# High weights that move the high and the low part of 256 tokens in one matmul of 512 columns

## The chip, the cores and the metric

The kernel runs on one core of one Trainium2 chip, in one launch. The metric is the device time in microseconds (us); lower is better. The engines that matter here are TensorE (PE; its weight loads are PEld in the profile), VectorE (DVE), ScalarE (ACT), and the DMA queue of SyncE (SP). Each engine works through its own list of instructions in order, and semaphores tie the lists together.

## The reference, cut to what matters

Two blocks of a transformer on 256 tokens (the second with 256 tokens of context beside them), D = 1024, in float32. The change concerns the two feed forwards that run on the 256 tokens alone: the one at the end of the first block, and the very last one of the program.

```python
def swiglu(xn, w_ffn_in, w_ffn_out):            # first block
    gate, up = jnp.split(xn @ w_ffn_in, 2, axis=-1)
    return (jax.nn.silu(gate) * up) @ w_ffn_out   # 1024 -> 2 x 2816 -> 1024
h = h + swiglu(rmsnorm(h, norm2_w), w_ffn_in, w_ffn_out)

# last feed forward of the second block
x = x + 0.5 * mx[8] * swiglu_2(modulate(rms_norm(x), mx[6], mx[7]), *ffn2)
```

The other feed forwards run on tokens and context together (512 columns).

## The kernel before

**Numbers in two parts.** Every operand of a large matmul is kept as a high part (rounded to the type fp32r) and a low part (the rest). A product is three matmuls into the same sums: high weights by high x, high weights by low x, low weights by high x (`product`, line 344). Each matmul has its own weight load.

**Weights.** All weights come in chunks of 512 KB, eight tiles of 128 x 128, in one stream through a ring of RING = 6 slots. SP loads chunk c+6 once TensorE has used chunk c (`load_chunk`, L286). ScalarE casts a chunk to its high part (`split_hi`, L292), then VectorE subtracts to get the low part (`split_lo`, L298). Both do this LEAD = 3 chunks ahead: in step i of a stage each engine first splits chunk i+3 and then reads the sums that end with chunk i. TensorE waits for `lo_ready` before a chunk.

**The feed forward.** `ffn` makes two stages. `FfnUp` has 44 blocks of 128 features, gate and up blocks in turn, each with eight k tiles, so one chunk makes one block: 44 chunks. `IntoResid` (down) has 8 blocks with 22 k tiles each: 22 chunks. So a feed forward is 66 chunks or 528 tiles, 1584 matmuls of 256 columns. The sums rotate over BANKS = 3 banks of psum: block b waits until the bank of block b-3 has been read.

**Reading the sums.** After a gate block ScalarE writes `raw = silu(psum)` (L571). After an up block VectorE multiplies, `raw = raw * psum` (L582), ScalarE casts that to the high part of the hidden tile (L574), and VectorE subtracts to the low part (L584). In the down part VectorE adds each of the eight blocks into `resid` (L439 without a gate, L446 with one), and then sums squares (L454 to L457).

**Which feed forwards.** With 256 tokens the tile set is `hidden_x`. The first one (feed forward 1 below) is interleaved, chunk by chunk, with the stage `Modulation(1)`: its own 512 KB chunks, matmuls on L715, and per round a ScalarE copy (L726), two transposes (L707) and a VectorE addition (L737). The last one (feed forward 2) stands alone near the end of the program; after it come transposes and the store of the result. The norm ahead of each writes `normed` tile by tile.

Of the kernel before, what the change touches and what calls it, by code (L numbers as in the profile page):

```python
# [13 lines left out]
P = 128  # L14
S = 256
# [153 lines left out]
def build(nc, W, consts, where, out):  # L169
    with ExitStack() as ctx:  # L170
# [6 lines left out]
        def raw_hi_lo(name, *free):  # L177

            start = -(-nc.sbuf_base // 32) * 32
            raw = sb(name + "_raw", *free)  # L180
            hi_at[name] = -(-nc.sbuf_base // 32) * 32
# [3 lines left out]
        hi_at = {}  # L185
# [18 lines left out]
        normed_raw, *normed = raw_hi_lo("normed", KD, 2 * S)  # L204
        under_hi = nc.alloc_sbuf_tensor_at("under_normed_hi", [P, KD, 2 * S], F32, offset=hi_at["normed"])
# [12 lines left out]
        hidden_x = [at(KF * S, KF, S), *split_at("hidden_x", (0, KF * S), KF, S)]  # L218
# [9 lines left out]
        def row(name):  # L228
# [33 lines left out]
                  "single": 0, "sub": 0, "evac_act": 0, "evac_dve": 0, "merged": 0}  # L262
# [84 lines left out]
        class LinearF(Stream):  # L347
# [8 lines left out]

            def tensor(self, pe, i):
                c = self.first + i
                pe.wait_ge(lo_ready, c + 1)
                for q in range(CT * i, CT * (i + 1)):  # L360
# [5 lines left out]
                    j = q % CT  # L366
                    last = self.product(psum[:, self.bank(b), 0:self.w], c, slice(j * P, (j + 1) * P), False,
# [54 lines left out]
        class IntoResid(LinearF):  # L422
# [11 lines left out]
            def evac_vector(self, dve, step, i):  # L434
                for k in self.ended(i):
                    dve.wait_ge(used, self.first + i + 1)
                    r = resid[:, k, self.a]
                    if self.gate is None:
# [113 lines left out]
        class FfnUp(LinearF):  # L552
# [7 lines left out]
            def parts(self, h):  # L560
                return [t[:, h, :] for t in self.pair]
# [4 lines left out]
            def evac_scalar(self, act, step, i):  # L566
                for b in self.ended(i):
                    raw, hi, _ = self.parts(b // 2)
# [7 lines left out]
            def evac_vector(self, dve, step, i):  # L576
                for b in self.ended(i):
                    raw, hi, lo = self.parts(b // 2)
                    if b % 2 == 1:
                        dve.wait_ge(*bank_free[self.group + b - 1])  # L580
                        dve.wait_ge(used, self.first + i + 1)
                        ve.tensor_tensor(raw, raw, self.sums(b), ALU.mult).then_inc(evac_dve, 1)  # L582
                        dve.wait_ge(hid_hi, self.hid0 + b // 2 + 1)
                        ve.tensor_tensor(lo, raw, hi.bitcast(F32), ALU.subtract).then_inc(hid_ready, 1)  # L584
# [1502 lines left out]
        def ffn(up, down, tiles, a, pair, gate, norm):  # L2087

            first = FfnUp(up, tiles, a, pair)
            first.ready = norm.ready  # L2090
            second = IntoResid(down, tiles, pair[1:], slice(0, a.stop - a.start), gate)
            second.ready = first.hidden_ready
# [324 lines left out]
```

## Time and profile before

| what | us |
|---|---|
| median of 3 runs | 2839.81 (2838.78 to 2842.81) |
| the profiled execution | 2841.48 |
| its span (first to last instruction) | 2839.7 |
| PE busy in the span | 2596.8 (91%) |
| DVE busy | 1378.9 (49%) |
| ACT busy | 1044.0 (37%) |
| granted TensorE clock, mean | 0.954 of full speed |
| feed forward 1, from its second chunk to its last matmul | about 592 to 829 |
| feed forward 2, likewise | about 2643 to 2831 |

The profile's page counts a matmul as busy from its start until its result has drained, so consecutive matmuls overlap in it. The distance between the starts of two matmuls is the better measure of what one costs in a stream. A line of a timeline reads: start, duration, engine, line of the kernel, operation, what is written and read, and in brackets the idle time before it with what ended it.

### The profile page before, as it was taken

To read this page: it belongs to the slowest core of one execution; us is meant where nothing else is said; L and a number is where in the kernel's file an instruction comes from. 1 tells how busy PE (TensorE), PEld (TensorE's weight loads), DVE (VectorE), ACT (ScalarE), POOL (GpSimd) and SP (SyncE) were. 2 spreads that over 40 slices of the span, in tenths; PEclk is the share of its full clock that TensorE was granted. 3 is DMA by queue.
4 is the path that set the end of the run, shared out by engine and by line. 5 is a ranking of instruction groups with operands and counts; after the bars stand their busy time and mean duration, and the time that the engine had idled before them with its cause. 6 is when DMAs were issued, how large, how long until landed. Compare 5 with 4: busy or idle time off the path is not lost. (4 is left out here: it accounts for less than half of the span.)

```text
span 2839.7 us, 36318 instructions
## 1 busy us (share of the span) xinstructions
PE 2596.8 (91%) x15294; PEld 2159.7 (76%) x15294; DVE 1378.9 (49%) x2279; ACT 1044.0 (37%) x1628; POOL 0.2 (0%) x4
## 2 busy tenths in 40 slices
PE   5999899899989999989888999989999896758999
PEld 5887679878867888867666888868888784446898
DVE  3746454554444333367865333343333354556654
ACT  3534454433333222245542222132222243344443
POOL 0000000000000000000000000000000000000000
PEclk8999999999999999989989999999999997769999
DMA  6886643488842222335002322322222243021454
GB/s 229 273 253 207 207 134 111 134 303 301 295 155 83 98 98 98 97 117 167 1 23 75 98 98 98 98 76 96 97 96 97 89 150 94 1 74 39 160 182 140
DMA packets 145188, 372.36 MB, mean 131 GB/s; under 512 B 20202, under 2 KB 65794, under 8 KB 144898
## 3 DMA queue, kind: packets, MB, share of 16 engines
q1 hardware_dynamic: 144402, 367.82, 40.2%
q8 instruction: 122, 2.00, 0.3%
q10 hardware_dynamic: 624, 2.21, 0.2%
q14 instruction: 40, 0.33, 0.0%
HBM read 368.84 MB, written 1.15 MB: 130 GB/s over the span
## 5 line engine op out<-in xcount | busy, mean ns | idle before, releaser
L298 DVE TENSOR_TENSOR weights_lo<-weights_raw,weights_hi 128x1024 fp32r<-128x1024 f32 (+1 forms) x545 | 656.1, 1216 | 536.0 <-ACT weights_hi L292 533.8
L344 PE MATMUL psum<-normed_hi,weights_hi 128*128 128x256 f32 (+1 forms) x2560 | 866.8, 339 | 38.5 <-DVE normed_lo L543 28.1
L344 PE MATMUL psum<-normed_lo,weights_hi 128*128 128x256 f32 (+1 forms) x2560 | 847.3, 331 | 0.0
L344 PE MATMUL psum<-normed_hi,weights_lo 128*128 128x256 f32 (+1 forms) x2560 | 846.7, 331 | 0.0
L292 ACT CAST weights_hi<-weights_raw 128x1024 fp32r<-128x1024 f32 (+1 forms) x545 | 562.0, 1039 | 382.3 <-DMA weights_raw<-in_w_down 267.3
L344 PEld LDWEIGHTS psum<-normed_hi,weights_hi 128*128 128x128 f32 x2560 | 488.7, 191 | 136.5 <-issue 67.3
L344 PEld LDWEIGHTS psum<-normed_lo,weights_hi 128*128 128x128 f32 x2560 | 490.0, 191 | 43.7 <-issue 1.2
L344 PEld LDWEIGHTS psum<-normed_hi,weights_lo 128*128 128x128 f32 x2560 | 489.4, 191 | 44.4
L344 PE MATMUL psum<-hidden_hi,weights_hi 128*128 128x512 f32 x528 | 205.4, 389 | 0.0
L344 PE MATMUL psum<-hidden_lo,weights_hi 128*128 128x512 f32 x528 | 205.4, 389 | 0.0
L344 PE MATMUL psum<-hidden_hi,weights_lo 128*128 128x512 f32 x528 | 205.4, 389 | 0.0
L344 PE MATMUL psum<-weights_hi,normed_hi 128*128 128x512 f32 (+2 forms) x400 | 151.4, 379 | 27.4 <-DVE weights_lo L298 14.9
L446 DVE SCALAR_TENSOR_TENSOR resid<-psum,mod,resid 128x256 f32<-128x256 f32 x80 | 35.8, 481 | 273.5 <-PE psum L344 273.5
L582 DVE TENSOR_TENSOR arena<-arena,psum 128x512 f32<-128x512 f32 (+1 forms) x110 | 63.9, 581 | 209.4 <-PE psum L344 209.4
L574 ACT CAST hidden_hi<-arena 128x512 fp32r<-128x512 f32 x66 | 40.9, 620 | 309.3 <-DVE arena L582 309.3
L571 ACT ACTIVATE arena<-psum 128x512 f32<-128x512 f32 (+1 forms) x110 | 56.3, 512 | 250.1 <-PE psum L344 250.0
L344 PE MATMUL psum<-weights_hi,normed_lo 128*128 128x512 f32 (+2 forms) x400 | 147.5, 369 | 0.0
L344 PE MATMUL psum<-weights_lo,normed_hi 128*128 128x512 f32 (+2 forms) x400 | 147.2, 368 | 0.0
L344 PEld LDWEIGHTS psum<-weights_hi,normed_hi 128*128 128x128 f32 x400 | 81.4, 204 | 46.6 <-issue 18.3
L344 PEld LDWEIGHTS psum<-hidden_hi,weights_lo 128*128 128x128 f32 x528 | 99.1, 188 | 20.7
L344 PEld LDWEIGHTS psum<-hidden_hi,weights_hi 128*128 128x128 f32 x528 | 99.1, 188 | 20.5
L344 PEld LDWEIGHTS psum<-hidden_lo,weights_hi 128*128 128x128 f32 x528 | 99.1, 188 | 20.5
(290 smaller groups left out, 2886.5 us busy)
## 6 DMA issues: line engine op xcount, KB each, us to landing
weights_raw<-in_w_gu SPq DMA_DIRECT2D x220, 512.0 KB, 3.5
weights_raw<-in_w_down SPq DMA_DIRECT2D x110, 512.0 KB, 3.5
arena<-in_w_mod SPq DMA_DIRECT2D x72, 512.0 KB, 5.5
resid<-in_w_mod SPq DMA_DIRECT2D x24, 512.0 KB, 5.2
normed_raw<-in_w_mod SPq DMA_DIRECT2D x24, 512.0 KB, 5.5
under_normed_hi<-in_w_mod SPq DMA_DIRECT2D x24, 512.0 KB, 5.3
weights_raw<-in_w_x SPq DMA_DIRECT2D x24, 512.0 KB, 4.5
weights_raw<-in_w_qk SPq DMA_DIRECT2D x24, 512.0 KB, 3.8
```

Of the source, the lines that this page charges most:

```text
L292: se.copy(w_hi[:, c % RING, a], w_raw[:, c % RING, a]).then_inc(hi_ready, 1)
L298: ve.tensor_tensor(w_lo[:, c % RING, a], w_raw[:, c % RING, a], w_hi[:, c % RING, a].bitcast(F32), ALU.subtract).then_inc(lo_ready, 1)
L344: last = te.matmul(out, a, b, start=start and n == 0, stop=stop and n == 2)
L446: last = ve.scalar_tensor_tensor(out=resid[:, k, mine], in0=psum[:, self.bank(k), side * S - at0:(side + 1) * S - at0], scalar=mod[:, m, s ...
L571: se.activation(raw, self.sums(b), ACT.Silu).then_inc(evac_act, 1)
L574: se.copy(hi, raw).then_inc(hid_hi, 1)
L582: ve.tensor_tensor(raw, raw, self.sums(b), ALU.mult).then_inc(evac_dve, 1)
```

## The change

In both feed forwards of 256 tokens, high and low part of x now lie side by side in memory (`normed_parts`, `hidden_parts`), and the high weights move both in one matmul of 2 x 256 columns. The low weights then move the high part alone (256 columns). Per tile there are two matmuls and two weight loads where there were three of each. The sums of a block therefore stand as two halves of one bank, to be added on the way out:

- Up part (`FfnUpHalves`): ScalarE copies one half to SBUF (`hid_half`), VectorE adds the other half (`evac_dve`). For a gate block ScalarE then applies silu to that sum (`hid_silu`). For an up block VectorE multiplies both (`hid_gate`), ScalarE casts the product to the high part, VectorE subtracts to the low part.
- Down part: two VectorE instructions for each block, one per half, with a wait between them, in place of one.

The feed forwards of 512 columns keep `FfnUp` and three matmuls. The layout of `normed` changes for all (low and high part of a k tile alternate), not what is read of it.

```diff
 # LinearF.tensor
+                    if self.parts is not None:
+                        a, bank = slice(j * P, (j + 1) * P), self.bank(b)
+                        te.matmul(psum[:, bank, :].rearrange("p (n t) -> p n t", n=2), w_hi[:, c % RING, a],
+                                  self.parts[:, k, :, self.a], start=k == 0, stop=False)
+                        last = te.matmul(psum[:, bank, 0:S], w_lo[:, c % RING, a], self.x[0][:, k, self.a],
+                                         start=False, stop=k == self.k_tiles - 1)
+                        continue
 # IntoResid.evac_vector
+                    if self.parts is not None:
+                        gate = 1.0 if self.gate is None else mod[:, (self.gate[0] * NMOD + self.gate[1]) * KD + k, 0:1]
+                        for half in range(2):
+                            last = ve.scalar_tensor_tensor(
+                                out=r, in0=psum[:, self.bank(k), half * S:(half + 1) * S], scalar=gate, in1=r,
+                                op0=ALU.mult, op1=ALU.add)
+                            if half == 0:
+                                step(last)
+        class FfnUpHalves(FfnUp):
...
+            def evac_scalar(self, act, step, i):
+                for b in self.ended(i):
+                    raw, hi, _ = self.tiles_of(b // 2)
+                    act.wait_ge(used, self.first + i + 1)
+                    se.copy(raw if b % 2 == 0 else hidden_up[:, b // 2, :], self.halves(b)[0]).then_inc(hid_half, 1)
+                    if b % 2 == 0:
+                        act.wait_ge(*bank_free[self.group + b])
+                        se.activation(raw, raw, ACT.Silu).then_inc(hid_silu, 1)
+                    else:
+                        act.wait_ge(hid_gate, self.silu0 + b // 2 + 1)
+                        se.copy(hi, raw).then_inc(hid_hi, 1)
+
+            def evac_vector(self, dve, step, i):
+                for b in self.ended(i):
+                    raw, hi, lo = self.tiles_of(b // 2)
+                    dve.wait_ge(hid_half, 2 * self.silu0 + b + 1)
+                    if b % 2 == 0:
+                        ve.tensor_tensor(raw, raw, self.halves(b)[1], ALU.add).then_inc(evac_dve, 1)
+                    else:
+                        up = hidden_up[:, b // 2, :]
+                        ve.tensor_tensor(up, up, self.halves(b)[1], ALU.add).then_inc(evac_dve, 1)
+                        dve.wait_ge(*bank_free[self.group + b])
+                        dve.wait_ge(hid_silu, self.silu0 + b // 2 + 1)
+                        ve.tensor_tensor(raw, raw, up, ALU.mult).then_inc(hid_gate, 1)
+                        dve.wait_ge(hid_hi, self.hid0 + b // 2 + 1)
+                        ve.tensor_tensor(lo, raw, hi.bitcast(F32), ALU.subtract).then_inc(hid_ready, 1)
```

What stands in a row on three engines, in the up part of feed forward 2. First TensorE, two tiles at the start of a block, before and then after:

```order
L344 MATMUL psum<-normed_hi,weights_hi 128x256 [waits banks_read_by_scalar,weights_lo_ready]
L344 MATMUL psum<-normed_lo,weights_hi 128x256
L344 MATMUL psum<-normed_hi,weights_lo 128x256
L344 MATMUL psum<-normed_hi,weights_hi 128x256
L344 MATMUL psum<-normed_lo,weights_hi 128x256
L344 MATMUL psum<-normed_hi,weights_lo 128x256
```

```order
L373 MATMUL psum<-normed,weights_hi 128x512 [waits banks_read_by_vector,weights_lo_ready]
L375 MATMUL psum<-normed,weights_lo 128x256
L373 MATMUL psum<-normed,weights_hi 128x512
L375 MATMUL psum<-normed,weights_lo 128x256
L373 MATMUL psum<-normed,weights_hi 128x512
L375 MATMUL psum<-normed,weights_lo 128x256
```

Three matmuls per tile became two; a block's bank is now always freed by VectorE.

Next ScalarE, from the reading of an up block through that of the next gate block and on to the next cast of weights. Before (L574 reads an up block, L571 a gate block):

```order
L574 CAST hidden_x_hi<-arena 128x256 [waits banks_read_by_vector]
L292 CAST weights_hi<-weights_raw 128x1024 [waits weights_landed_4]
L571 ACTIVATE arena<-psum 128x256 [waits weights_used]
L292 CAST weights_hi<-weights_raw 128x1024 [waits weights_landed_5]
L574 CAST hidden_x_hi<-arena 128x256 [waits banks_read_by_vector]
L292 CAST weights_hi<-weights_raw 128x1024 [waits weights_landed_0]
```

After (L294 is the cast of weights that was L292; L623 copies a half, L629 is the cast of the hidden tile, L626 the silu). The rows begin with the cast of weights of an up block's step:

```order
L294 CAST weights_hi<-weights_raw 128x1024 [waits weights_landed_1]
L623 COPY arena<-psum 128x256 [waits weights_used]
L629 CAST hidden_x<-arena 128x256 [waits hidden_product_ready]
L294 CAST weights_hi<-weights_raw 128x1024 [waits weights_landed_2]
L623 COPY arena<-psum 128x256 [waits weights_used]
L626 ACTIVATE arena<-arena 128x256 [waits banks_read_by_vector]
L294 CAST weights_hi<-weights_raw 128x1024 [waits weights_landed_3]
```

Each step of ScalarE now has a copy that waits for TensorE and then an instruction that waits for VectorE, in both kinds of steps; the next cast of weights stands behind it.

Last VectorE, a gate block's step and an up block's step. Before (`x2` is one split for each of the two steps):

```order
L298 TENSOR_TENSOR weights_lo<-weights_raw,weights_hi 128x1024 [waits weights_hi_ready] x2
L582 TENSOR_TENSOR arena<-arena,psum 128x256 [waits weights_used,banks_read_by_scalar]
L584 TENSOR_TENSOR hidden_x_lo<-arena,hidden_x_hi 128x256 [waits hidden_hi_ready]
L298 TENSOR_TENSOR weights_lo<-weights_raw,weights_hi 128x1024 [waits weights_hi_ready] x2
```

After (L300 was L298; L636 and L639 add the halves, L642 multiplies, L644 makes the low part):

```order
L300 TENSOR_TENSOR weights_lo<-weights_raw,weights_hi 128x1024 [waits weights_hi_ready]
L636 TENSOR_TENSOR arena<-arena,psum 128x256 [waits hidden_first_half_copied]
L300 TENSOR_TENSOR weights_lo<-weights_raw,weights_hi 128x1024 [waits weights_hi_ready]
L639 TENSOR_TENSOR arena<-arena,psum 128x256 [waits hidden_first_half_copied]
L642 TENSOR_TENSOR arena<-arena 128x256 [waits hidden_silu_ready,banks_read_by_vector]
L644 TENSOR_TENSOR hidden_x<-arena,hidden_x 128x256 [waits hidden_hi_ready]
L300 TENSOR_TENSOR weights_lo<-weights_raw,weights_hi 128x1024 [waits weights_hi_ready]
```

Between the two splits there is now an addition that waits for ScalarE's copy, and behind the second split an addition, the multiplication and the low part.

## Rows read from the trace of the kernel before

**Rows 1.** the page: span, busy time and share of each engine, instructions.

```profile
span 2839.7 us, 36318 instructions
...
PE 2596.8 (91%) x15294; PEld 2159.7 (76%) x15294; DVE 1378.9 (49%) x2279; ACT 1044.0 (37%) x1628; POOL 0.2 (0%) x4
```

**Rows 2.** stretches: length, busy (count) of PE, PEld, DVE, ACT, POOL; clock, DMA, GB/s.

```profile
680.00:700.00 20.00, 20.00 (x182) 17.10 (x181) 8.95 (x13) 7.26 (x12) 0.00 (x0) 1.00 0.87 282
...
2600.00:2620.00 20.00, 17.36 (x135) 15.57 (x134) 12.62 (x25) 7.49 (x10) 0.00 (x0) 1.00 0.24 79
...
2680.00:2700.00 20.00, 20.00 (x169) 20.00 (x168) 11.51 (x15) 9.13 (x14) 0.00 (x0) 1.00 0.56 181
```

**Rows 3.** timeline, TensorE, feed forward 2: start us, duration us, line.

```profile
2643.44 0.28 PE L344 MATMUL psum<-normed_hi,weights_hi 128*128 128x256 f32 x1
...
2767.28 0.28 PE L344 MATMUL psum<-hidden_x_hi,weights_hi 128*128 128x256 f32 x1
...
2830.52 0.28 PE L344 MATMUL psum<-hidden_x_hi,weights_lo 128*128 128x256 f32 x1
```

**Rows 4.** timeline, TensorE, a stretch with 512 columns.

```profile
1119.80 0.39 PE L344 MATMUL psum<-hidden_hi,weights_hi 128*128 128x512 f32 x1
...
1138.84 0.39 PE L344 MATMUL psum<-hidden_hi,weights_hi 128*128 128x512 f32 x1
```

**Rows 5.** timeline, VectorE, feed forward 2, up part.

```profile
2704.19 0.42 DVE L582 TENSOR_TENSOR arena<-arena,psum 128x256 f32<-128x256 f32 x1 [0.38 <-PE psum L344]
2705.09 0.43 DVE L584 TENSOR_TENSOR hidden_x_lo<-arena,hidden_x_hi 128x256 fp32r<-128x256 f32 x1 [0.47 <-ACT hidden_x_hi L574]
2706.03 1.22 DVE L298 TENSOR_TENSOR weights_lo<-weights_raw,weights_hi 128x1024 fp32r<-128x1024 f32 x1 [0.52 <-ACT weights_hi L292]
```

**Rows 6.** timeline, ScalarE, the same stretch.

```profile
2701.52 1.04 ACT L292 CAST weights_hi<-weights_raw 128x1024 fp32r<-128x1024 f32 x1
2704.64 0.41 ACT L574 CAST hidden_x_hi<-arena 128x256 fp32r<-128x256 f32 x1 [2.09 <-DVE arena L582]
2704.96 1.04 ACT L292 CAST weights_hi<-weights_raw 128x1024 fp32r<-128x1024 f32 x1
```

**Rows 7.** timeline, the start of feed forward 2, ScalarE, then VectorE.

```profile
2642.31 1.03 ACT L292 CAST weights_hi<-weights_raw 128x1024 fp32r<-128x1024 f32 x1
2643.36 1.28 ACT L571 ACT_TABLE_LOAD   x1
...
2643.38 1.23 DVE L298 TENSOR_TENSOR weights_lo<-weights_raw,weights_hi 128x1024 fp32r<-128x1024 f32 x1 [0.45 <-ACT weights_hi L292]
2646.01 1.22 DVE L298 TENSOR_TENSOR weights_lo<-weights_raw,weights_hi 128x1024 fp32r<-128x1024 f32 x1 [1.41 <-ACT weights_hi L292]
2647.15 0.41 DVE L582 TENSOR_TENSOR arena<-arena,psum 128x256 f32<-128x256 f32 x1
```

**Rows 8.** timeline, feed forward 1: TensorE's up part, then ScalarE.

```profile
592.50 0.39 PE L344 MATMUL psum<-normed_hi,weights_hi 128*128 128x256 f32 x1
...
750.42 0.39 PE L344 MATMUL psum<-hidden_x_hi,weights_hi 128*128 128x256 f32 x1
...
706.99 0.37 ACT L726 COPY arena<-psum 128x256 f32<-128x256 f32 x1
707.25 1.05 ACT L292 CAST weights_hi<-weights_raw 128x1024 fp32r<-128x1024 f32 x1
```

**Rows 9.** who waited for whom, 600 to 825 us (total us, times, longest).

```profile
ACT weights_hi L292 <- DMA weights_raw<-in_w_gu: 3.2, 2, 2.5
```

**Rows 10.** timeline, VectorE, the ends of both feed forwards.

```profile
828.80 0.42 DVE L439 TENSOR_TENSOR resid<-resid,psum 128x256 f32<-128x256 f32 x1 [2.02 <-PE psum L344]
...
2825.60 0.42 DVE L456 TENSOR_TENSOR squares<-resid 128x256 f32<-128x256 f32 x1
2826.06 0.43 DVE L457 TENSOR_TENSOR squares<-squares 128x256 f32<-128x256 f32 x1
...
2830.91 0.48 DVE L446 SCALAR_TENSOR_TENSOR resid<-psum,mod,resid 128x256 f32<-128x256 f32 x1 [4.42 <-PE psum L344]
```

More of the change, by code:

```diff
@@ L217, in build @@
         hidden = [at(KF * 512, KF, 512), *split_at("hidden", (0, KF * 512), KF, 512)]
-        hidden_x = [at(KF * S, KF, S), *split_at("hidden_x", (0, KF * S), KF, S)]
+        hidden_parts = nc.alloc_sbuf_tensor_at("hidden_x", [P, KF, 2, S], F32R, offset=arena_at)
+        hidden_up, hidden_raw = (at(0, KF * 2, S).rearrange("p (k n) s -> p n k s", n=2)[:, n] for n in range(2))
+        hidden_x = [hidden_raw, *(hidden_parts[:, :, n, :] for n in range(2))]
         def C(name):
@@ L355, in __init__ @@
                 self.groups(evacs or ["evac_act"] * blocks)
+            parts = None
             def tensor(self, pe, i):
@@ L582, in evac_vector, with __init__, halves @@
                         ve.tensor_tensor(raw, raw, self.sums(b), ALU.mult).then_inc(evac_dve, 1)
+                        dve.wait_ge(hid_hi, self.hid0 + b // 2 + 1)
+                        ve.tensor_tensor(lo, raw, hi.bitcast(F32), ALU.subtract).then_inc(hid_ready, 1)
+        hid_half, hid_silu, hid_gate = (
+            sem("hidden_" + n) for n in ("first_half_copied", "silu_ready", "product_ready"))
+        class FfnUpHalves(FfnUp):
+            def __init__(self, weights, tiles, a, pair):
+                LinearF.__init__(self, weights, KD, 2 * tiles, normed, a, None, evacs=["evac_dve"] * (2 * tiles))
+                self.pair, self.parts = pair, normed_parts
+                self.hid0, self.silu0 = take("hidden", tiles), take("silu", tiles)
+            def halves(self, b):
+                return [psum[:, self.bank(b), half * S:(half + 1) * S] for half in range(2)]
+            def evac_scalar(self, act, step, i):
+                for b in self.ended(i):
+                    raw, hi, _ = self.tiles_of(b // 2)
+                    act.wait_ge(used, self.first + i + 1)
[8 more added lines that the diff above has]
+                for b in self.ended(i):
+                    raw, hi, lo = self.tiles_of(b // 2)
+                    dve.wait_ge(hid_half, 2 * self.silu0 + b + 1)
[7 more added lines that the diff above has]
+                        ve.tensor_tensor(raw, raw, up, ALU.mult).then_inc(hid_gate, 1)
                         dve.wait_ge(hid_hi, self.hid0 + b // 2 + 1)
@@ L2087, in ffn @@
         def ffn(up, down, tiles, a, pair, gate, norm):
-            first = FfnUp(up, tiles, a, pair)
+            first = (FfnUpHalves if pair is hidden_x else FfnUp)(up, tiles, a, pair)
             first.ready = norm.ready
             second = IntoResid(down, tiles, pair[1:], slice(0, a.stop - a.start), gate)
+            if pair is hidden_x:
+                second.parts = hidden_parts
             second.ready = first.hidden_ready
```

17 lines of the change are left out of this document (8 added, 9 removed).

## The prediction

> **What bounds the kernel now.** I read the page's first part: TensorE is busy for 91% of the span [rows 1]. An average says little, so I looked at stretches inside the two feed forwards of 256 tokens. In both, TensorE is busy for 20.00 of 20 us at a granted clock of 1.00 [rows 2]; VectorE and ScalarE are busy for 11.5 and 9.1 of 20 in feed forward 2. The reader should then look at distances of starts, not at durations. In feed forward 2, from the first matmul of chunk 1 to the first of the down part, 43 chunks (1032 matmuls) take 2767.28 - 2643.44 = 123.84 us [rows 3]: 120.0 ns for one of 256 columns. The down part goes on at that rate to 2830.52. With 512 columns, 84 distances take 19.04 us [rows 4]: 226.7 ns. At 2.4 GHz 256 columns stream in 106.7 ns and 512 in 213.3 ns. So each matmul with its weight load has the same fixed part, 13.3 ns, at both widths. That fixed part is all there is to win: the number of columns streamed per tile stays 768.
>
> **What the matmuls give.** A tile costs 3 x 120.0 = 360.0 ns before and 226.7 + 120.0 = 346.7 ns after: 13.3 ns less. A chunk of eight tiles goes from 2.88 to 2.773 us, two chunks (a gate and an up block, "a pair" below) from 5.76 to 5.547 us. The two feed forwards have 1056 tiles: 14.1 us if TensorE stays the bound in both.
>
> **What reading the sums costs.** The additions lie beside the matmuls as busy time. What matters is the order. ScalarE's step is now: cast the weights of chunk i+3, copy a half, wait for VectorE, then silu or cast. VectorE's step is: split chunk i+3 (needs that cast), add the other half, and for an up block multiply. ScalarE's next cast of weights stands behind its wait for VectorE, in every step, and VectorE's addition stands behind its own split. So cast, split, addition, silu or cast, next cast form a closed chain through both engines. Its length per pair, from starts:
> - cast to split: 2704.96 to 2706.03, 1.07 us [rows 5, 6];
> - split to an addition that needn't wait: 2646.01 to 2647.15, 1.14 [rows 7];
> - addition on psum to ScalarE's start: 2704.19 to 2704.64, 0.45 [rows 5, 6];
> - ScalarE's cast of a hidden tile to the next cast of weights: 0.32 [rows 6]; I take the same for silu.
>
> A gate step is 1.07 + 1.14 + 0.45 + 0.32 = 2.98 us. In an up step the addition is followed by the multiplication with a wait for its own engine, 0.46 (2825.60 to 2826.06, the same pattern [rows 10]), and the multiplication hands over after another 0.46 (0.43 as L584, plus the 0.03 between 2704.61 and 2704.64 [rows 5, 6]): 1.07 + 1.14 + 0.46 + 0.46 + 0.32 = 3.45. A pair is 6.43 us. ScalarE's copy of a half fits beside the split, the low part beside the next cast, so neither counts. Before, the gate step had no wait for VectorE: ScalarE went from silu straight on, and the chain per pair held one split, not two; the 2.09 us that ScalarE idled ahead of L574 [rows 6] were cover.
>
> The Trainium skill says the same of the queues: by the page "TensorE: Matmul & The Clock Gate", section "Architectural detail: the array is 16× 32×32, not 1× 128×128", ScalarE and VectorE are strict first in, first out, and TensorE alone can pull a weight load ahead. This speaks against the change, and rows 6 agree, in that a cast of weights that starts 0.32 us behind L574 had waited with it.
>
> **Feed forward 1.** TensorE shares it with the modulation. Chunk 1 starts at 592.50, the down part at 750.42 [rows 8]: 157.92 / 43 = 3.673 us per chunk, 3.566 after, 7.13 a pair. The chain is 6.43 plus the modulation's copy on ScalarE, 0.26 [rows 8] once in some eight chunks, so about 6.5: it stays covered by 0.6 us a pair. Weights: ScalarE waited for gate and up weights twice, 3.2 us in all [rows 9], and the DMA share of 0.87 [rows 2] rises to 0.90 at the new pace, still hidden. So the full gain: 528 x 13.3 ns = -7.0 us. At the end the last block has two additions with a wait between: 0.48 + 0.04 + 0.48 in place of 0.42 [rows 10], +0.6 us on the path to the next norm.
>
> **Feed forward 2.** Nothing slows TensorE there, and 6.43 is more than 5.547: after a few pairs TensorE waits for VectorE in every chunk. The start [rows 7]: the first split of the loop starts at 2643.38, the addition 1.14 later at 2644.52. ScalarE's copy waits for chunk 0 (to about 2643.6), takes 0.38, then comes the load of the silu table, 1.28: silu at 2645.34, the next cast of weights at 2645.66. From that step (1) to step 43 are 21 pairs: 2645.66 + 21 x 6.43 = 2780.69. Chunk 46 needs its low weights and a free bank, so the addition of step 43: + 1.07 + 1.14 + 0.42 + 0.03 = 2783.35. Before, chunk 46 began at 2643.44 + 45 x 2.88 = 2773.04. So TensorE is 10.3 us late by then, 15.2 us behind its own new pace (21 x (6.43 - 5.547) = 18.6, of which the lead of three chunks absorbs 3.3: chunk 4 could start at 2648.3 by the chain and does by the matmuls at 2651.7). The last 20 chunks are down chunks, whose splits wait for nobody: -20 x 0.107 = -2.1. The split for chunk 47 comes 0.3 late behind the last low part. Together +8.5, and 0.5 for the second addition at the very end [rows 10], ahead of the transposes: +9.0 us.
>
> **Sum:** -7.0 + 0.6 + 9.0 = +2.6, rounded to +2.5 for the tenths cut above. The profiled execution took 2841.48 us, 1.7 above the median; against the median the forecast is 2839.8 + 2.5 = 2842.3 us. The profile's span would go from 2839.7 to about 2842.2.
>
> **Bounds.** The chain's terms are rows of the same shapes; what no row shows is the multiplication's two semaphores, silu out of SBUF, and both engines this closely coupled. Ends: 0.2 less a pair if the four handoffs (0.03 or 0.04 each in these rows) and the tails of two instructions overlap fully, 0.2 more if each of the four costs 0.05 more. 21 pairs make that -4 and +5 us. I take 6.43, made of measured distances. For the two-part moving operand the fixed part is 13.3 ns by both widths; it could cost a little more or less, -3 to +3 us over feed forward 1. Together about 2837 to 2848.
>
> **Rivals.**
> - *All is hidden.* If ScalarE and VectorE overlapped so that a pair took under 5.55 us, the gain would be whole: -14.1 + 1.1 = -13.0, 2826.8 us. For it: the busy shares, 11.5 and 9.1 of 20 [rows 2], to which the additions and copies put some 3 us each. Against: the chain above, whose every link is a semaphore or an engine's order.
> - *The chain reaches feed forward 1 too* (the slower side). Should a pair take 7.0 to 7.2 us, because handoffs between the two engines cost more when neither has slack, feed forward 2 loses 21 x 0.6 = 12 us more, and feed forward 1, whose pairs last 7.13, begins to lose its gain, some 2 us: 2842.3 + 14 = 2856 us. It decides from 7.13 on. For it: the margin is only 0.6 us, and the modulation puts ScalarE and VectorE behind TensorE once a round. Against: the links are measured.
> - *The fixed part isn't won.* The wide matmul reads two runs of 256 columns from separate places, and if that costs the 13.3 ns again, or most of it, feed forward 1 saves 1.3 instead of 7.0, and the down chunks of feed forward 2 lose 1.7: 2842.3 + 7.4 = 2849.7 us. By the page "TensorE: Matmul & The Clock Gate", section "Back-to-back issue gap", a warm matmul is N / 2.4 + 2.5 ns, and a matmul less would save just 2.5 ns; rows 3 and 4 show 13.3, and they decide.
> - *The clock falls.* TensorE will idle about 0.44 us in each chunk of feed forward 2. At the lower level a chunk would last 5.3 us or so, longer than the chain's 3.2, and each 10 us of it would cost 4 us. Against: 2600 to 2620 us, with 17.36 busy of 20, shows a clock of 1.00 [rows 2].
>
> **How the numbers follow.** Forecast 0.55, all hidden 0.15, chain in both 0.20, fixed part not won 0.07, clock 0.03. The range 2835 to 2858 holds the forecast with its bounds, the chain in both and the fixed part, 0.82, and leaves out the other two. What this kernel's measurement can tell from no change is about 0.2%, 5.7 us: 2834.1 to 2845.5 is "same". The forecast's own 2837 to 2848 lies in it for 0.44 of its 0.55; the rest, 0.11, with 0.20, 0.07 and 0.03 is slower, 0.41; faster is 0.15.
>
> **What the profile after would show.** Right: in feed forward 2's up part TensorE busy less than before, idle ahead of the first matmul of nearly every chunk on an addition or split of VectorE, some 0.45 us; casts of weights 2.98 and 3.45 us apart in turn; in its down part and in the wide tiles 346.7 ns a tile; in feed forward 1 TensorE still without gaps for VectorE, and its up part 4.6 us shorter. Wrong: casts 5.55 us a pair apart (all hidden), a pair above 7 us, a tile of about 357 ns, or a clock below 1.00 in feed forward 2.

## The result and the profile after

The changed kernel is slower by a little: 2848.8 us median against 2840.53, a ratio of 1.0029 (95% interval 1.0022 to 1.0037), about 8 us. A later series of the same kernel gave 1.0031 (1.0020 to 1.0042). The forecast was 2842.3 us with a range of 2835 to 2858; the likeliest verdict there was no change (0.44), slower had 0.41. The interval here leaves out 1.0000, so the loss is real, and it is small.

The page of the profiled execution, which took 2855.49 us; it answers [rows 1]:

```profile
span 2853.4 us, 34398 instructions
...
PE 2607.4 (91%) x14238; PEld 2103.9 (74%) x14238; DVE 1417.6 (50%) x2383; ACT 1073.8 (38%) x1716; POOL 0.2 (0%) x4
```

1056 matmuls fewer (15294 to 14238), as the change says, and VectorE and ScalarE busier by 38.7 and 29.8 us in sum. Next the stretches that answer [rows 2]: length, busy time of PE, PEld, DVE, ACT and POOL with counts, granted clock, DMA share, GB/s.

```profile
680.00:700.00 20.00, 20.00 (x139) 14.73 (x138) 11.25 (x17) 9.94 (x17) 0.00 (x0) 1.00 0.85 296
...
2680.00:2700.00 20.00, 18.79 (x101) 15.27 (x102) 11.89 (x18) 10.49 (x20) 0.00 (x0) 1.00 0.47 161
...
2800.00:2820.00 20.00, 20.00 (x115) 17.36 (x114) 12.54 (x16) 7.36 (x7) 0.00 (x0) 1.00 0.54 185
```

In feed forward 1 (680 to 700) TensorE is still never idle. In feed forward 2's up part (2680 to 2700) it is idle for 1.2 us of 20 where it had been busy throughout, at a clock of 1.00; in the down part (2800 to 2820) it is full again. The page counts a matmul until it has drained, so the idle time is larger than that. It shows in who waited for whom in feed forward 2, 2652 to 2845 us: who, for whom, us in all, times, longest.

```profile
PEld psum L373 <- DVE weights_lo L300: 11.6, 18, 0.7
PE psum L373 <- DVE arena L636: 6.0, 15, 0.4
```

Before, the up part (2655 to 2767 us) had no wait of TensorE of its own that the same view lists. The chain behind it, on ScalarE, answers [rows 6] (start, duration, engine, line; L629 casts a hidden tile, L294 weights, L623 copies a half, L626 is the silu):

```profile
2708.94 0.41 ACT L629 CAST hidden_x<-arena 128x256 fp32r<-128x256 f32 x1 [1.81 <-DVE arena L642]
2709.25 1.05 ACT L294 CAST weights_hi<-weights_raw 128x1024 fp32r<-128x1024 f32 x1
2710.20 0.36 ACT L623 COPY arena<-psum 128x256 f32<-128x256 f32 x1
2711.92 0.42 ACT L626 ACTIVATE arena<-arena 128x256 f32<-128x256 f32 x1 [1.35 <-DVE arena L636]
2712.24 1.04 ACT L294 CAST weights_hi<-weights_raw 128x1024 fp32r<-128x1024 f32 x1
...
2715.36 0.41 ACT L629 CAST hidden_x<-arena 128x256 fp32r<-128x256 f32 x1 [1.82 <-DVE arena L642]
```

And on VectorE, answering [rows 5] (L300 splits weights, L636 and L639 add halves, L642 multiplies, L644 makes the low part):

```profile
2706.89 1.23 DVE L300 TENSOR_TENSOR weights_lo<-weights_raw,weights_hi 128x1024 fp32r<-128x1024 f32 x1 [1.42 <-ACT weights_hi L294]
2708.03 0.41 DVE L639 TENSOR_TENSOR arena<-arena,psum 128x256 f32<-128x256 f32 x1
2708.48 0.42 DVE L642 TENSOR_TENSOR arena<-arena 128x256 f32<-128x256 f32 x1
2709.38 0.42 DVE L644 TENSOR_TENSOR hidden_x<-arena,hidden_x 128x256 fp32r<-128x256 f32 x1 [0.47 <-ACT hidden_x L629]
2710.33 1.23 DVE L300 TENSOR_TENSOR weights_lo<-weights_raw,weights_hi 128x1024 fp32r<-128x1024 f32 x1 [0.53 <-ACT weights_hi L294]
2711.47 0.41 DVE L636 TENSOR_TENSOR arena<-arena,psum 128x256 f32<-128x256 f32 x1
```

From cast of weights to cast of weights: 2709.25 to 2712.24 is 2.99 us (the gate step), and from L629 to L629, 2708.94 to 2715.36, a pair takes 6.42 us. The links are those of the forecast: 2709.25 to 2710.33 (1.08), 1.14 to the addition, 0.45 to the silu, 0.32 to the next cast; 2708.03, 2708.48, 2708.94 for addition, multiplication, cast.

What a tile costs: the first and the last wide matmul of 113 consecutive distances in feed forward 2's down part, where nothing waits:

```profile
2800.03 0.40 PE L373 MATMUL psum<-hidden_x,weights_hi 128*128 128x512 f32 x1
...
2839.96 0.40 PE L373 MATMUL psum<-hidden_x,weights_hi 128*128 128x512 f32 x1
```

39.93 us / 113 = 353.4 ns a tile; forecast were 346.7, before it was 360.0 ([rows 3], three matmuls of 120.0).

**Time by stage.** All from starts in the timelines: feed forward 1 from the first matmul of chunk 1 to its last; feed forward 2 from its first split of weights behind the norm (2643.38 in [rows 7]) to the first matmul of its down part, and from there to its last; then to the end of the span.

| stage, us | before | after | forecast change | measured |
|---|---|---|---|---|
| feed forward 1 | 235.98 | 232.51 | -7.0 | -3.5 |
| from there to the last matmul of the middle feed forwards | 1432.84 | 1433.06 | +0.6 | +0.2 |
| from there (norm, attention of the second layer) to feed forward 2 | 382.06 | 388.77 | 0 | +6.7 |
| feed forward 2, up | 123.90 | 133.36 | +9.6 | +9.5 |
| feed forward 2, down | 63.24 | 63.16 | -1.1 | -0.1 |
| from the last matmul to the end | 9.18 | 11.12 | +0.5 | +1.9 |

The forecasts for up and down stand behind the sum of the text: by its terms the down part could begin 133.5 us after the first split, 9.6 later than before, and all of feed forward 2 was +8.5. The +0.6 of the second row is the second addition at the end of feed forward 1. What lies ahead of the first row ended some 1 us earlier than before (chunk 1 at 591.45 in place of 592.50). The third row, 6.7 us in stages that the change doesn't touch, was not forecast; the experiments come back to it.

### The profile page after: what moved, and what is told of

Same layout as the page of the kernel before. It is cut to its first block and busy times, and to the rows that moved or that the text cites. A ratio compares the mean times of both kernels' runs of the same rounds, so it can differ in the third digit from the quotient of the medians.

```text
span 2853.4 us, 34398 instructions
## 1 busy us (share of the span) xinstructions
PE 2607.4 (91%) x14238; PEld 2103.9 (74%) x14238; DVE 1417.6 (50%) x2383; ACT 1073.8 (38%) x1716; POOL 0.2 (0%) x4
## 5 line engine op out<-in xcount | busy, mean ns | idle before, releaser
L346 PE MATMUL psum<-normed,weights_hi 128*128 128x512 f32 (+1 forms) x3712 | 977.1, 352 | 30.7 <-DVE normed L562 23.6
L300 DVE TENSOR_TENSOR weights_lo<-weights_raw,weights_hi 128x1024 fp32r<-128x1024 f32 (+1 forms) x545 | 655.8, 1216 | 530.5 <-ACT weights_hi L294 528.1
L346 PEld LDWEIGHTS psum<-normed,weights_hi 128*128 128x128 f32 x3712 | 651.4, 190 | 155.2 <-issue 45.7
L294 ACT CAST weights_hi<-weights_raw 128x1024 fp32r<-128x1024 f32 (+1 forms) x545 | 561.2, 1038 | 373.0 <-DMA weights_raw<-in_w_down 259.3
L346 PE MATMUL psum<-normed,weights_lo 128*128 128x512 f32 (+1 forms) x1856 | 646.8, 348 | 0.0
L346 PEld LDWEIGHTS psum<-normed,weights_lo 128*128 128x128 f32 x1856 | 353.5, 190 | 44.1
L373 PE MATMUL psum<-normed,weights_hi 128*128 128x512 f32 x704 | 261.3, 411 | 13.9 <-DVE arena L636 6.0
L346 PE MATMUL psum<-weights_hi,normed 128*128 128x512 f32 (+2 forms) x800 | 229.3, 374 | 27.5 <-DVE weights_lo L300 15.0
L375 PE MATMUL psum<-normed,weights_lo 128*128 128x256 f32 x704 | 197.9, 281 | 0.0
L346 PEld LDWEIGHTS psum<-weights_hi,normed 128*128 128x128 f32 x800 | 150.4, 203 | 57.4 <-issue 18.3
L373 PEld LDWEIGHTS psum<-normed,weights_hi 128*128 128x128 f32 x704 | 133.0, 189 | 69.7 <-issue 21.2
L346 PE MATMUL psum<-weights_lo,normed 128*128 128x512 f32 (+2 forms) x400 | 147.2, 368 | 0.0
L375 PEld LDWEIGHTS psum<-normed,weights_lo 128*128 128x128 f32 x704 | 134.1, 191 | 0.0
L373 PE MATMUL psum<-hidden_x,weights_hi 128*128 128x512 f32 x352 | 127.2, 404 | 0.4 <-DVE weights_lo L300 0.4
```

The lines of the kernel that those rows point to most:

```text
L294: se.copy(w_hi[:, c % RING, a], w_raw[:, c % RING, a]).then_inc(hi_ready, 1)
L300: ve.tensor_tensor(w_lo[:, c % RING, a], w_raw[:, c % RING, a], w_hi[:, c % RING, a].bitcast(F32), ALU.subtract).then_inc(lo_ready, 1)
L346: last = te.matmul(out, a, b, start=start and n == 0, stop=stop and n == 2)
L373: te.matmul(psum[:, bank, :].rearrange("p (n t) -> p n t", n=2), w_hi[:, c % RING, a], self.parts[:, k, :, self.a], start=k == 0, stop=False)
L375: last = te.matmul(psum[:, bank, 0:S], w_lo[:, c % RING, a], self.x[0][:, k, self.a], start=False, stop=k == self.k_tiles - 1)
```

## The experiments

Times are given as the ratio to the kernel before, which ran on the same chip in the same series; a time without a ratio is a single run. A stage is as defined for the table above, and stage times come from one profiled execution of each kernel.

**Opening the chain** (e1_defer). The instruction that waits for VectorE goes one step later on ScalarE; the low part likewise on VectorE.

```diff
 # FfnUpHalves.evac_scalar: silu or cast of block b-1 ahead of the copy of block b
...
+                    if b:
+                        self.finish_scalar(act, b - 1)
                     act.wait_ge(used, self.first + i + 1)
                     se.copy(raw if b % 2 == 0 else hidden_up[:, b // 2, :], self.halves(b)[0]).then_inc(hid_half, 1)
-                    if b % 2 == 0:
-                        act.wait_ge(*bank_free[self.group + b])
-                        se.activation(raw, raw, ACT.Silu).then_inc(hid_silu, 1)
-                    else:
-                        act.wait_ge(hid_gate, self.silu0 + b // 2 + 1)
-                        se.copy(hi, raw).then_inc(hid_hi, 1)
+                    if b == self.blocks - 1:
+                        self.finish_scalar(act, b)
...
```

> The changed kernel, with ScalarE's silu or cast of block b-1 (which waits for VectorE) moved one step later, behind the next cast of weights and ahead of the next copy, and the low part moved likewise. Same instructions, same lead. Theory (closed chain of cast, split, addition, silu or cast): the chain is open, TensorE no longer waits in the up part of feed forward 2, whose 43 chunks take 43 x 8 x 353 ns = 121.5 us in place of 133.4, and the time falls by 10 to 12 us against the changed kernel, to some 2836 or less, 4 to 7 us below the kernel before. Rival (the idle time comes from a lack of busy-time room, or from the wide matmuls themselves): the work is the same, so feed forward 2 stays about as long and the time stays near 2849.

Measured: 0.9970 (0.9960 to 0.9980), 2832.2 us. Feed forward 2: up 121.60 us (expected 121.5), down 62.08. ScalarE in the same place:

```profile
2705.80 0.37 ACT L634 COPY arena<-psum 128x256 f32<-128x256 f32 x1 [1.11 <-PE psum L375]
2706.07 1.05 ACT L294 CAST weights_hi<-weights_raw 128x1024 fp32r<-128x1024 f32 x1
2707.02 0.42 ACT L623 ACTIVATE arena<-arena 128x256 f32<-128x256 f32 x1
2708.62 0.37 ACT L634 COPY arena<-psum 128x256 f32<-128x256 f32 x1 [1.18 <-PE psum L375]
2708.89 1.05 ACT L294 CAST weights_hi<-weights_raw 128x1024 fp32r<-128x1024 f32 x1
2709.94 0.41 ACT L626 CAST hidden_x<-arena 128x256 fp32r<-128x256 f32 x1
2711.45 0.37 ACT L634 COPY arena<-psum 128x256 f32<-128x256 f32 x1 [1.10 <-PE psum L375]
```

Now silu (L623) and cast (L626) start as soon as the cast of weights before them allows it, with no idle time in brackets; ScalarE idles only for TensorE. Of its waits for VectorE in this feed forward one is left (the last block):

```profile
ACT hidden_x L626 <- DVE arena L651: 0.9, 1, 0.9
```

The same instructions in another order are 16 us faster than the changed kernel by the medians and 12.8 us shorter in feed forward 2. So neither busy time nor the wide matmuls made the loss in feed forward 2, but the closed chain.

The repeat (e1_defer_again):

> The kernel of e1_defer again, beside the two others, since its gain of 9 us was measured with five to nine runs: the sum by stages gives -7.4 us against before (-4.4 in feed forward 1, -3.5 in feed forward 2, +0.5 at the end), 2833; a repeat should lie between 2830 and 2836.

Measured: 0.9972 (0.9964 to 0.9981), 2831.7 us, within the expected 2830 to 2836. It beats both kernels: the changed one had 2849.4 us in the same series.

**Feed forward 1 alone** (e3_ff1_only). `FfnUpHalves` and the wide matmuls only where `gate is None`.

> Halves in feed forward 1 only; feed forward 2 as before. Theory: feed forward 1 is bound by TensorE, its chain is covered, and it gains what the trace of the changed kernel shows there, 4 to 4.5 us: about 2836 to 2837. Rival (the chain reaches feed forward 1 too): no gain or a loss there, 2840 or more.

Measured: 0.9997 (0.9988 to 1.0006), 2842.5 us. The time was a miss: no gain that can be told from zero. The stage was not: feed forward 1 took 232.50 us, 3.5 less than before, and feed forward 2 187.14, exactly as before. In its profile the attention stretch ahead of feed forward 2 took 385.67 us (before 382.06) and the end 10.93 (9.18), together more than the gain.

**Feed forward 2 alone** (e6_ff2_only).

> Halves in feed forward 2 only; feed forward 1 as before. Theory: all of the loss sits here, +9.4 us inside feed forward 2 and 0.5 to 2 us behind it: 2850 to 2852, slower than the changed kernel. Rival (the loss beyond the forecast comes from elsewhere, for example the new layout of normed in the stages between): 2845 or less.

Measured: 1.0040 (1.0028 to 1.0052), 2853.7 us (five runs), above the expected 2850 to 2852; the interval, 2849.9 to 2856.7 us, covers it. Feed forward 2: 133.37 and 63.18 us, +9.4 in all, feed forward 1 as before (235.98). So the loss inside the changed parts is feed forward 2's. The end took 12.84 us in this profile, 3.7 more than before, where 0.5 to 2 were expected.

**The down parts alone** (e4_down_only). `FfnUp` in both, `second.parts` kept.

> Wide matmuls in the two down parts only, up parts with three matmuls and one reading instruction for each block, as before. Theory: no chain, 353 ns a tile instead of 360 in 352 tiles, -2.4 us, and the second addition at both ends, +1.1: about -1.3 us, 2839. If the fixed part were fully won (346.7 ns a tile), -4.7 + 1.1 = -3.6 us, 2837. Rival (wide matmuls are no cheaper at all): +1 us.

Measured: 1.0002 (0.9993 to 1.0010), 2844.6 us in place of the expected 2839: the time was a miss. Down parts 76.55 and 62.07 us in place of 78.06 and 63.24, 353.3 ns a tile in the second: -1.5 and -1.2, -2.7 in all (expected -2.4). With 0.5 for each second addition the stages would give -1.7 us, and the time does not show it: 6 of these 11 runs had a mean granted clock of 0.951 or less, and they are the slower ones (2844.6 to 2845.3 us against 2840.1 to 2842.6). The last experiment comes back to this clock.

**A longer chain** (e7_two_more_links). Two more awaited multiplications in each up block's step:

```diff
+                        for _ in range(2):
+                            step(ve.tensor_tensor(squares[:, 1, 0:S], raw, up, ALU.mult))
                         ve.tensor_tensor(raw, raw, up, ALU.mult).then_inc(hid_gate, 1)
```

> The changed kernel with two more multiplications on VectorE into a scratch tile, each awaited, between the addition and the product of every up block: 2 x 0.46 us more in the chain for each pair. Theory (closed chain): a pair in feed forward 2 takes 6.42 + 0.92 = 7.34 us, so feed forward 2 is 21 x 0.92 = 19.3 us longer than with the changed kernel; and feed forward 1, whose pairs last some 7.05 us, is now bound by the chain too and longer by 4 to 8 us. Rival (only busy time counts): VectorE still has room, 5.6 of 6.4 us, and both feed forwards change by less than 3 us.

Measured: 2880.2 us. A pair in feed forward 2, from cast to cast on ScalarE:

```profile
2710.56 0.41 ACT L629 CAST hidden_x<-arena 128x256 fp32r<-128x256 f32 x1 [2.73 <-DVE arena L644]
...
2717.89 0.41 ACT L629 CAST hidden_x<-arena 128x256 fp32r<-128x256 f32 x1 [2.73 <-DVE arena L644]
```

7.33 us (expected 7.34); feed forward 2 took 215.66 us, 19.1 more than with the changed kernel (expected 19.3). Feed forward 1 took 240.84, 8.3 more (expected 4 to 8). This is the forecast's threshold: a chain above the pace of feed forward 1, some 7.1 us a pair, binds there too. Its pairs are 7.33 to 7.61 us long in 20 of 21 cases, 13 of them 7.33 or 7.34 as in feed forward 2. The one left took 12.34 us, where it is 8.89 in the changed kernel. There TensorE waited for the modulation's copy on ScalarE (L788), which stands behind the awaited cast, and in the 4 us after this wait (628 to 632) the granted clock was 0.50:

```profile
627.73 0.69 PE L769 MATMUL psum<-const,arena 128*128 128x128 f32 x2 [3.76 <-ACT arena L788]
```

VectorE had room in busy time in both (132.28 of 220 us from 600 to 820, 85.11 of 130 from 2670 to 2800).

**More lead** (e8_lead4). `LEAD = 4`.

> The changed kernel with weights split four chunks ahead instead of three. Theory (closed chain): its length doesn't depend on the lead, a pair stays at 6.42 us, and feed forward 2 gains one step at most, about 3 us, since the bank of block b-3 still waits for the same addition. Rival (too little lead to ride out latencies): with one chunk more, TensorE's waits in feed forward 2 vanish and it is 9 to 12 us shorter than with the changed kernel.

Measured: 2849.0 us. A pair is unchanged, 6.41 us:

```profile
2705.68 0.41 ACT L629 CAST hidden_x<-arena 128x256 fp32r<-128x256 f32 x1 [1.82 <-DVE arena L642]
...
2712.09 0.41 ACT L629 CAST hidden_x<-arena 128x256 fp32r<-128x256 f32 x1 [1.81 <-DVE arena L642]
```

Up 133.28 us (133.36), down 61.45 (63.16): 1.8 us less, no more than the step that was allowed for. Some 1.0 us of it has nothing to do with the lead: in the down part this execution ran its last 153 tiles at 346.7 ns instead of 353.3 (rows below, under "The same kernel, two tiles"). The gain didn't reach the whole either: feed forward 1 began 5.3 us later than in the changed kernel (596.70 against 591.45). The lead is not what is short.

**Grouped widths** (e2_defer_group, e5_group_only). To find why a tile costs 353 and not 347 ns: eight wide matmuls of a chunk, then eight narrow ones, first with the open chain, then with the closed one.

```diff
+                    for wide in (True, False):
+                        for q in range(CT * i, CT * (i + 1)):
...
```

> The kernel of e1_defer, with the eight wide matmuls of a chunk first and its eight narrow ones behind them. Theory A (the fixed part grows because widths alternate): wide tiles cost 226.7 and narrow ones 120.0 ns as in streams of one width, 346.7 a tile in place of 353.3; 1056 tiles give 7 us more than e1_defer, about 2825 to 2826. Theory B (the fixed part of the wide matmul itself is larger, whatever its neighbours): 353 ns a tile stays, 2832. Theory C (the weight load hides less well under narrow matmuls): wide ones drop to 226.7, narrow ones stay as dear as in a stream of their own, 120, which is theory A's number too; the starts of wide and narrow matmuls tell by how much each changes.

> The changed kernel with its matmuls grouped as in e2_defer_group, the chain as it was. Feed forward 2 is bound by the chain, not by TensorE: its up part should stay at 6.42 us a pair whatever a tile costs, 133.4 us from its first split to the down part give or take 0.5; feed forward 1 would be 3.5 us shorter by theory A, unchanged by theory B.

Measured: 1.0001 (0.9991 to 1.0011) with the open chain. TensorE there (start, duration, eight matmuls a row):

```profile
2690.98 2.00 PE L375 MATMUL psum<-normed,weights_hi 128*128 128x512 f32 x8
2692.82 1.12 PE L378 MATMUL psum<-normed,weights_lo 128*128 128x256 f32 x8
2693.78 2.00 PE L375 MATMUL psum<-normed,weights_hi 128*128 128x512 f32 x8
```

Wide ones are (2.00 - 0.39) / 7 = 230.0 ns apart, narrow ones (1.12 - 0.28) / 7 = 120.0; a chunk takes 2.80 us, 350 ns a tile. That lies between the theories: neither 346.7 nor 353.3. The time was expected at 2825 to 2826 or 2832 and came out at 2842.6 us, behind the kernel of e1_defer; in its profile feed forward 1 and 2 are together within a microsecond of that kernel, and the attention stretch took 388.76 us. Nine of its 12 runs had a mean granted clock of 0.951 or less. With the closed chain (2848.9 us) the up part of feed forward 2 took 135.41 us, above the 133.4 give or take 0.5 that was expected. The pairs are as before (splits at 2654.68 and 2661.09, 6.41 us); the 2 us are lost at the start, where the second split came 5.21 us behind the first in place of 3.34. Feed forward 1 was 0.7 us shorter (its last narrow matmul counted), not 3.5. So grouping is no gain here.

**One run of 512 columns** (e10_flat_down). Operand and sums of the down parts' wide matmul written as one run.

> The kernel of e2_defer_group, where in the down parts operand and sums of the wide matmul are written as one run of 512 columns instead of two of 256 (the same addresses in the same order). If the pattern of two runs costs the 3.3 ns by which a wide matmul there (230.0) exceeds one in the feed forwards of 512 columns (226.7), the down part of feed forward 2 falls by 176 x 3.3 ns = 0.6 us and wide ones stand 226.7 apart. If not, 230.0 stays. Time: as e2_defer_group, within 1 us.

Measured: 0.9990 (0.9980 to 1.0000), 2837.7 us. That is 5 us below e2_defer_group, which ran in another series on another chip, so "within 1 us" was a miss; 6 of its 11 runs had a mean granted clock of 0.951 or less, there it was 9 of 12. The stage decides: the down part of feed forward 2 is the same to 0.01 us as in e2_defer_group, and the rows too:

```profile
2792.37 2.00 PE L380 MATMUL psum<-hidden_x,weights_hi 128*128 128x512 f32 x8
2794.21 1.12 PE L382 MATMUL psum<-hidden_x,weights_lo 128*128 128x256 f32 x8
2795.17 2.00 PE L380 MATMUL psum<-hidden_x,weights_hi 128*128 128x512 f32 x8
```

230.0 ns again. The way the operand is written is not the cause.

**The same kernel, two tiles.** The repeat of e1_defer answers part of it. In its first profile, feed forward 2's up part, 112 distances between wide matmuls:

```profile
2700.30 0.40 PE L373 MATMUL psum<-normed,weights_hi 128*128 128x512 f32 x1
...
2739.87 0.40 PE L373 MATMUL psum<-normed,weights_hi 128*128 128x512 f32 x1
```

39.57 us / 112 = 353.3 ns. In the second profile of the same program, 114 distances:

```profile
2700.20 0.39 PE L373 MATMUL psum<-normed,weights_hi 128*128 128x512 f32 x1
...
2739.72 0.39 PE L373 MATMUL psum<-normed,weights_hi 128*128 128x512 f32 x1
```

39.52 / 114 = 346.7 ns, and this held for all of feed forward 2 (up 119.31 us, down 60.90), while feed forward 1 was as in the first (231.59 against 231.55). So a tile of a wide and a narrow matmul has two paces, 6.7 ns apart, with no change in the program.

The pace can also change inside one execution, and then at a wait of TensorE. In the profile of LEAD = 4, in the down part of feed forward 2, 19 distances and, after a pause of 0.25 us (the next wide matmul came 0.60 us behind the last), 153 more:

```profile
2776.27 0.40 PE L373 MATMUL psum<-hidden_x,weights_hi 128*128 128x512 f32 x1
...
2782.98 0.40 PE L373 MATMUL psum<-hidden_x,weights_hi 128*128 128x512 f32 x1
...
2784.03 0.40 PE L373 MATMUL psum<-hidden_x,weights_hi 128*128 128x512 f32 x1
...
2837.07 0.39 PE L373 MATMUL psum<-hidden_x,weights_hi 128*128 128x512 f32 x1
```

6.71 / 19 = 353.2 ns, then 53.04 / 153 = 346.7. In the first profile of the changed kernel, whose TensorE waits ahead of each chunk, 34 chunks in a row from 2680 to 2788 us have one pace each: 353.3 in 19, 346.7 in 15. Where TensorE doesn't wait, all 519 distances of feed forward 2 are of one kind (e1_defer and its repeat). The forecast's 346.7 exists; of the eight profiles with this mix of widths, the long last stretch of feed forward 2 has 353.3 in five and 346.7 in three.

**The stretch that nobody touched** (e9_after_again). The changed kernel once more:

> The changed kernel once more, for a second profile. If the 6.7 us that the first profile shows between the feed forward of the second block's first layer and feed forward 2, in attention stages that the change doesn't touch, come from the granted clock of that execution (0.51 against 0.76 in 2411 to 2460 us), they need not return: that stretch takes 380 to 389 us in any kernel, and its length goes with its clock. If they come from the new layout of normed, they stay at 388 us or more. The two feed forwards should repeat to 0.3 us: 155.9 and 76.6, 133.4 and 63.2.

Measured: 1.0031 (1.0020 to 1.0042). Feed forward 1 232.56, feed forward 2 133.69 and 63.18 us, within 0.4 of the first profile. The stretch ahead of it took 381.94 us, 6.8 less than in the first profile and as much as before (382.06). It goes with the granted clock: 2411 to 2460 us before, then in the first and the second profile of the changed kernel (columns as above, the granted clock is the third from the end):

```profile
2411.00:2460.00 49.00, 37.94 (x144) 21.35 (x143) 28.22 (x77) 15.62 (x34) 0.00 (x0) 0.76 0.00 1
```

```profile
2411.00:2460.00 49.00, 46.64 (x132) 25.66 (x130) 22.62 (x63) 13.19 (x28) 0.00 (x0) 0.51 0.00 0
```

```profile
2411.00:2460.00 49.00, 41.77 (x153) 23.64 (x151) 26.65 (x74) 14.59 (x31) 0.00 (x0) 0.71 0.00 0
```

0.76, 0.51 and 0.71; in this attention TensorE is idle in between, and for how much of it the lower of the two levels is granted varies. The new layout of `normed` costs nothing there. The other profiles agree: with 0.50 to 0.58 in these 49 us the stretch took 388.8 to 389.0 us (five profiles), with 0.69 to 0.90 it took 379.7 to 385.7 (nine), the kernel before and the changed one among them. In this second profile the parts sum to the whole: the span went from 2839.70 to 2844.91, +5.2, of which feed forward 1 -3.4, feed forward 2 +9.7, the end +0.5, what lies ahead of feed forward 1 -1.8 and the rest +0.2.

Last, the kernel before, as an experiment of its own (e11_before_again):

> The kernel before, unchanged, to see how its own executions spread. The stage sum of the changed kernel's second profile gives +5.2 us against the first profile of before, the medians +8 to +9. If the rest is only the granted clock in the attention stages, whose low phases fall in some executions of any kernel, then executions of before with a mean clock of 0.949 to 0.951 should be found too, at 2847 us or more, beside those of 0.954 at 2838 to 2841. If before has none, the changed kernel meets the low clock more often, for a reason not known.

Measured: 1.0001 (0.9992 to 1.0010); eleven runs from 2838.6 to 2843.3 us with mean clocks of 0.952 to 0.957, none lower. In the two series of e1_defer and of its repeat before did show 0.950 and 0.951, at 2845.0 to 2848.4 us, in 5 of 51 runs, and in no other series (93 runs in all whose clock was noted); the changed kernel has mean clocks of 0.951 or less in 11 of 29, at 2851.0 to 2855.5 us. So the expected spread exists in both, but the changed kernel meets it more often. Comparing runs of like clock takes this out: at 0.954 and more the changed kernel runs 2844.9 to 2848.0 us, median 2846.1, before 2835.7 to 2843.0, median 2839.9: +6.1 us. At 0.951 and less the medians are 2853.6 and 2847.0: +6.6 us. So some 6 of the 8 us are there at like clock, as the stages say, and some 2 go with the more frequent low clock.

## Why the prediction was right or wrong

- **What bounds (right).** The closed chain through ScalarE and VectorE was found in the order of the instructions and priced from rows: 6.43 us a pair, measured 6.42. The busy shares would have said that all is hidden.
- **Feed forward 2 (right).** The down part was to begin 133.5 us after the first split and began at 133.36 to 133.69. The step that failed in part is what comes behind: by the tile of 346.7 ns the last 20 chunks gain 2.1 us, by the measured one half of that; so +9.4 in place of +8.5.
- **Feed forward 1 (direction right, size wrong).** The term "528 x 13.3 ns = -7.0" was mis-sized: the stage gained 3.5 us. Of the missing 3.5 some 2.6 are the tile's: with the open chain the stage gained 4.4 us, 8.4 ns a tile, between the 6.7 and 13.3 that the two paces give. The other 1.0 is the chain's. "It stays covered" was nearly right: TensorE did wait there for splits, 17 times by the waits from 600 to 825 us, where it had waited three times before, and once for the modulation's copy (L786), which stands behind the awaited cast of the hidden tile on ScalarE:

```profile
PEld psum L373 <- DVE weights_lo L300: 7.0, 17, 0.4
```

```profile
625.05 0.44 PE L767 MATMUL psum<-const,arena 128*128 128x128 f32 x2 [1.52 <-ACT arena L786]
```

With the open chain this wait is 0.49 us and the stage 231.55 us instead of 232.51, so the chain took 1.0 us. The forecast counted the modulation's copy as 0.26 us of ScalarE's time and not as an instruction that TensorE waits for.

- **The fixed part (wrong).** "Each matmul has the same fixed part, 13.3 ns" was read from streams of one width. Mixed, a wide and a narrow one cost 33.3 ns beyond their columns (353.3 - 320) at one pace and 26.7 at the other. The rival "the fixed part isn't won" was half true. The bound that I gave (-3 to +3 us) was too narrow by a little. The page "TensorE: Matmul & The Clock Gate" of the Trainium skill, section "Back-to-back issue gap", gives a warm matmul by itself N / 2.4 + 2.5 ns. By that a matmul less would save 2.5 ns a tile; no run here shows that, the runs show 6.7 and 13.3. The same section of the Trainium skill keeps this formula for isolated matmuls and not for streams with weight loads, so it was no fair rival here.
- **The two ends (right).** A second addition costs 0.5 us at either end: from the last matmul to the end 9.68 to 9.70 us in eight profiles, 9.18 before, and behind feed forward 1 the addition takes 0.88 us in place of 0.42 (0.6 was forecast). In the first profile of the changed kernel the end was 11.12: both additions, and then 16 transposes that took 3.61 us at a granted clock of 0.53, where they had taken 1.97 at 1.00 before.

```profile
2842.70 1.00 DVE L452 SCALAR_TENSOR_TENSOR resid<-psum,mod,resid 128x256 f32<-128x256 f32 x2 [3.79 <-PE psum L375]
2844.72 3.61 PE L1548 MATMUL psum<-const,resid 128*128 128x128 f32 x16 [2.13 <-DVEq L2346]
```

- **Not foreseen.** By stages, with the attention's clock as before, the changed kernel is 5 to 6 us slower, and by runs of like clock 6; by medians 8 to 9. The rest goes with the granted clock of attention stages. The forecast treated the time outside the feed forwards as fixed, and its own range of 2837 to 2848 missed the median by a microsecond for this and for the tile. The stated range of 2835 to 2858 held the median only because it also covered the two slower rivals, and neither came true as it was priced; that is in part luck. The sum was +2.5, and what is missing from it is the tile (some 3.5 us in both feed forwards), the chain in feed forward 1 (1.0) and the granted clock outside them (some 2). The rival "the clock falls" named the wrong place: in feed forward 2's up part it stayed at 1.00 (2680 to 2700 us) with TensorE idle in every chunk.

Open: what sets a tile's pace to 346.7 or 353.3 ns after a wait, and why the changed kernel meets the lower mean clocks more often. Other variants do so too (the down parts alone 6 of 11 runs, the grouped widths 9 of 12), feed forward 1 alone hardly (1 of 10). A shift of a few us of the stages ahead of the attention could do it; no run shows that.

## What to carry to other kernels

When two engines hand work to each other, write down the order on both and look for a closed loop through an instruction that waits; its length per round is a bound, whatever the busy shares and the lead are. If such a loop is the bound, move the instruction that waits one round later: here that turned a loss of 0.3% into a gain of 0.3%, with no work changed. And a gain of a few nanoseconds a matmul, read from streams of one width, needs a measurement of the mix before it is multiplied by a thousand.

## What the runs showed of the hardware

- A stream that alternates matmuls of 512 and 256 columns runs at 353.3 or at 346.7 ns a tile. The pace holds as long as TensorE doesn't wait (519 tiles in e1_defer), can be the other one after a wait (e8_lead4 in one execution, 19 and 15 of 34 chunks in the changed kernel), and can differ between two executions of one program.
- In groups of eight, matmuls of 512 columns start 230.0 ns apart here, where the feed forwards of 512 columns show 226.7 ([rows 4]); writing the operand as one run changes nothing.
- TensorE kept its upper clock level through feed forward 2's up part with idle time in each chunk (1.00 from 2655 to 2775 us), and had a granted clock of 0.50 in the 4 us after one wait of 3.76 us (e7_two_more_links). The same 49 us of attention had a mean clock of 0.51 to 0.76 in three profiles of two kernels.
